# Chunk-wise loads of the activations in the last stage, with vector-engine additions and rows in another order

## What is computed

```python
top_s, top_pos = lax.top_k(cand_s, PEER_TOPK)
expert = jnp.take_along_axis(cand_i, top_pos, axis=-1)
gate = jax.nn.softmax(top_s, axis=-1)
ue = u[expert]
ve = v[expert]
act = jax.nn.gelu(jnp.einsum('thkd,td->thk', ue, ht))
return jnp.einsum('thk,thkd->td', gate * act, ve)
```

## Time and profile before

| | us |
|---|---|
| median of 3 runs | 2850.15 |
| lowest, highest run | 2846.03, 2854.32 |
| the profiled execution | 2851.25 |
| its span | 2849.5 |
| PE busy (95% of the span) | 2694.0 |
| DVE busy (72%) | 2065.5 |
| POOL busy (50%) | 1415.5 |
| ACT busy (32%) | 904.6 |

### The profile page before, as it was taken

The page is one execution under the profiler, slowest core; times in us unless marked ns, Lnnn a source line. Parts: engine busy times, 40 slices in busy tenths (PEclk is TensorE's granted clock), DMA queues, the critical chain, the costliest instruction groups (busy, mean ns, idle before and its releaser), DMA issues.

```text
span 2849.5 us, 43062 instructions
## 1 busy us (share of the span) xinstructions
PE 2694.0 (95%) x15691; PEld 2359.4 (83%) x15691; DVE 2065.5 (72%) x4758; ACT 904.6 (32%) x1750; POOL 1415.5 (50%) x960
## 2 busy tenths in 40 slices
PE   7999979998999999999999999979999998999998
PEld 6776658998999999999999999757767776777776
DVE  6022263699888989999999953668787777778774
ACT  4222341322222222356666622312222222222222
POOL 1111030446566677765565565535565554656640
PEclk9999989999999999999999999989999999999999
DMA  3101031436777888899999999989999999999993
GB/s 140 45 30 30 23 121 51 126 116 224 247 273 258 285 280 275 281 334 381 382 377 377 384 342 332 340 308 358 349 369 359 330 365 326 352 368 358 354 331 135
DMA packets 301905, 763.34 MB, mean 268 GB/s; under 512 B 22992, under 2 KB 138064, under 8 KB 298960
## 3 DMA queue, kind: packets, MB, share of 16 engines
q0 software_dynamic: 110592, 402.70, 38.4%
q1 hardware_dynamic: 191184, 359.13, 36.6%
HBM read 669.47 MB, written 92.27 MB: 267 GB/s over the span
## 4 chain that ended last, share of the span: by engine, by line
PE 54%; DVE 19%; issue 7%; DMA 4%; POOL 2%; ACT 1%; another core or an unknown queue 0%; SPq 0%; DVEq 0%; ACTq 0%
PE bank L1537 22%; PE bank L1881 20%; PE bank L1845 5%; DVE u_row L1332 4%; DMA g_raw<-g_d 3%; PE bank L1773 2%; PE bank L1756 2%; DVE yg L1467 2%; DVE y L1440 1%; PE wide L1901 1%; POOL w_lo L622 1%; DVE prod L1420 1%; DVE rest_k L1259 1%; DVE ix L1262 1%; DVE eq L1319 1%
## 5 line engine op out<-in xcount | busy, mean ns | idle before, releaser
L1537 PE MATMUL bank<-h_hi,w_hi 128*128 128x320 f32 (+1 forms) x2400 | 574.4, 321 | 16.4 <-POOL w_lo L622 12.8
L1537 PE MATMUL bank<-h_hi,w_lo 128*128 128x320 f32 (+1 forms) x2400 | 557.5, 314 | 0.0
L1537 PE MATMUL bank<-h_lo,w_hi 128*128 128x320 f32 (+1 forms) x2400 | 557.1, 313 | 0.0
L622 POOL TENSOR_TENSOR w_lo<-w_raw,w_hi 128x1024 fp32r<-128x1024 f32 x144 | 368.2, 2557 | 336.1 <-ACT w_hi L910 280.7
L1332 DVE CUSTOM_DVE_ANT_0 u_row<-wide,u_row 128x1024 f32<-128x1024 f32 x384 | 450.3, 1221 | 80.1 <-DMA u_row<-in_u_rows,ids 73.2
L684 POOL DMA_INDIRECT d_row<-in_v,ids x256 | 368.2, 1438 | 277.3 <-DVE yg L1467 231.6
L1881 PE MATMUL bank<-v_hi,a_hi 128*128 128x512 f32 x1272 | 408.1, 403 | 73.2 <-DVE y L1440 59.9
L631 POOL DMA_INDIRECT u_row<-in_u_rows,ids x384 | 391.3, 1019 | 111.5 <-issue 76.8
L1537 PEld LDWEIGHTS bank<-h_hi,w_hi 128*128 128x128 f32 x2400 | 401.1, 190 | 22.9 <-POOL w_lo L622 14.6
L1537 PEld LDWEIGHTS bank<-h_lo,w_hi 128*128 128x128 f32 x2400 | 406.7, 189 | 3.9
L1537 PEld LDWEIGHTS bank<-h_hi,w_lo 128*128 128x128 f32 x2400 | 405.5, 189 | 3.9
(11 more groups left out here) (213 smaller groups left out, 3682.5 us busy)
## 6 DMA issues: line engine op xcount, KB each, us to landing
w_raw<-in_u SPq DMA_DIRECT2D x128, 512.0 KB
v_raw<-in_v SPq DMA_DIRECT2D x128, 512.0 KB
act_d<-act_st SPq DMA_DIRECT2D x128, 320.0 KB
g_d<-g_st SPq DMA_DIRECT2D x20, 2048.0 KB
a_raw<-act_d SPq DMA_DIRECT2D x32, 768.0 KB
g_raw<-g_d SPq DMA_DIRECT2D x32, 768.0 KB
w_raw<-in_w_q SPq DMA_DIRECT2D x32, 512.0 KB
a_raw<-act_d SPq DMA_DIRECT2D x32, 512.0 KB
```

The lines of the kernel that those rows point to most:

```text
L622: nc.gpsimd.tensor_tensor(w_lo[:, s % 2, :], w_raw[:, s % 2, :], w_hi[:, s % 2, :], ALU.subtract).then_inc(lo_done, 1)
L1537: ins = pe.matmul(banks[h][:, 0:n], lhs[:, part], rhs[:, k, h * n:(h + 1) * n], start=(k == 0 and lhs is lhs_hi and rhs is h_hi), stop=(k ...
```

## The change

It has four parts, all in the second product.

1. `a_raw` is now eight places of one chunk each, in the same memory as the two places of four chunks before. `load_a(n)` loads the activations of product n alone, when product n - 8 has been gated (`pd_done`), and signals its own semaphore. `gated(n)` waits for that semaphore, and once for four chunks for the gates. The gates still come four chunks at a time. Instead of 64 loads there are 256.
2. SP's list: the five loads of `y` go from ahead of the stage to behind the first unit of group 0, and of each group's last four loads of `v` two more go ahead of the last unit.
3. `add_half` goes from the end of DVE's iteration n % 8 == 2 to the place right behind `lower_a(n)`.
4. Rows of `d_row`: in place of an even spread, `ROWS_PRODUCT` gives the number for each of a group's 16 iterations, 17 in all, 7 in iterations 0 to 7 and 10 in 8 to 15. POOL's gathers follow the same function.

```diff
+ROWS_PRODUCT = (0, 0, 0, 1, 1, 2, 2, 1, 2, 2, 0, 2, 2, 1, 0, 1)
+AR = 8
...
 def rows_added(n):
-    return min(max((n - 3) * VT * P // (HALVES * GT - 20), 0), VT * P)
+    full, m = divmod(n, 2 * GT)
+    return min(max(full * sum(ROWS_PRODUCT) + sum(ROWS_PRODUCT[:m]) - ROWS_PRODUCT[0], 0), VT * P)
...
-        a_raw = [at(f"a_raw{s}", 186 + 6 * s, [P, VJ, WA]) for s in range(2)]
+        a_raw = at("a_raw", 186, [P, AR, WA])
...
             def load_a(n):
-                j, w, s = GT * (n // 4) + VJ * (n % 2), half_width(n // 2), n % 2
-                t0 = n // 2 % 2 * WA
-                sp.dma_start(a_raw[s][:, :, 0:w], act_d[j:j + VJ, :, t0:t0 + w]
-                             .rearrange("j p t -> p j t")).then_inc(a_in[s], 16)
+                h, j = n // GT, GT * (n // (2 * GT)) + n % GT
+                w, t0 = half_width(h), h % 2 * WA
+                if n >= AR:
+                    sp.wait_ge(pd_done, n - AR + 1)
+                sp.dma_start(a_raw[:, n % AR, 0:w], act_d[j, :, t0:t0 + w]).then_inc(a_in[n % AR], 16)
...
-            def load_unit(n):
-                sp.wait_ge(pd_done, VJ * (n - 1))
-                load_a(n)
-                load_g(n)
+            def load_products(n0):
+                for n in range(n0, n0 + VJ):
+                    load_a(n)
+                sp.wait_ge(pd_done, n0 - VJ)
+                load_g(n0 // VJ)
...
             sp.wait_ge(uh_gate, 1)
-            for i in range(DT):
-                sp.dma_start(y[i][:, :], x1_d[i]).then_inc(y_in, 16)
             sp.wait_ge(row_used, ROWS)
...
-                load_unit(4 * g + 2)
-                load_unit(4 * g + 3)
+                n0 = 2 * GT * g
+                load_products(n0 + 2 * VJ)
+                if g == 0:
+                    for i in range(DT):
+                        sp.dma_start(y[i][:, :], x1_d[i]).then_inc(y_in, 16)
+                load_products(n0 + 3 * VJ)
                 for j in more[:VJ]:
                     load_v(j)
                 if more:
-                    load_unit(4 * g + 4)
-                for j in more[VJ:VR]:
+                    load_products(n0 + 4 * VJ)
+                for j in more[VJ:]:
                     load_v(j)
                 if more:
-                    load_unit(4 * g + 5)
-                for j in more[VR:]:
-                    load_v(j)
+                    load_products(n0 + 5 * VJ)
...
                 if n % VJ == 0:
-                    dve.wait_ge(a_in[s], 16 * (n // (2 * VJ) + 1))
                     dve.wait_ge(g_in[s], 16 * (n // (2 * VJ) + 1))
+                dve.wait_ge(a_in[n % AR], 16 * (n // AR + 1))
...
                 lower_a(n)
+                h = n // GT
+                if n % GT == 2 and h:
+                    if h == 1:
+                        dve.wait_ge(y_in, 16 * DT)
+                    for q in range(TT[(h - 1) % 2]):
+                        add_half(h - 1, q)
                 done = n - RA - 1
...
                     add_row(k)
-                h = n // GT
-                if n % GT == 2 and h:
-                    if h == 1:
-                        dve.wait_ge(y_in, 16 * DT)
-                    for q in range(TT[(h - 1) % 2]):
-                        add_half(h - 1, q)
```

More of the change, by code:

```diff
@@ L351, in build @@
         yd_done = sem("yd_done")
-        a_in = [sem("a_in0"), sem("a_in1")]
+        a_in = [sem(f"a_in{k}") for k in range(AR)]
         g_in = [sem("g_in0"), sem("g_in1")]
@@ L562, in _ @@
                     sp.wait_ge(act_out[1], 16 * GT // 2)
-                    load_a(k - 2)
+                    for n in range(VJ * (k - 2), VJ * (k - 1)):
+                        load_a(n)
                 elif k == 4:
@@ L1420, in gated @@
                 V.tensor_tensor(prod[:, n % 2, 0:w].rearrange("p (b t) -> p b t", t=TW),
-                                a_raw[s][:, j, 0:w].rearrange("p (b t) -> p b t", t=TW),
+                                a_raw[:, n % AR, 0:w].rearrange("p (b t) -> p b t", t=TW),
                                 g_raw[s][:, 0:w // TW, j * TW:(j + 1) * TW], ALU.mult).then_inc(pd_done, 1)
```

## The result

The change made the kernel slower: 2864.28 us median (2859.57 to 2872.29, 8 runs) against 2849.76 us of the kernel before (2846.03 to 2856.52, 8 runs), a ratio of 1.0045 with a 95% interval of 1.0031 to 1.0058. The prediction said 2798 us and gave "slower" 0.12. The profiled execution of the change took 2865.24 us, its span is 2863.5 us.

A forecast was written before the change was run, and what follows sets the result against it. PE sets the second product's pace, stalled by DVE's late additions, with the DMA limit near. Groups going from 64.25 to 60.8 us give 48 us over 14, with group 0 53 us: 2851.25 to 2798 us, range 2766 to 2842.

The forecast's parts named there:

- Part 3 (with part 4), additions behind `a_lo`: Second product, group starts: PE's stall and low clock go, 5.2 us for each of 14 groups, 73 us.
- PE's floor: Second product: groups take 59 us, bound by PE alone; as a rival 2772 us, chance 0.18.
- The lateness of the gates, put at nothing: Second product: late gates cost little, 3.58 us once in the steady groups and 13.3 in group 0; 0 us counted.
- Part 2, SP's list: Second product: 5 us gained in group 0; two earlier `v` loads cost 0 to 2 us a group, taken as 0.
- Part 1, chunk-wise loads: Second product's activations: gates arrive 3 us sooner and the hole at 139 GB/s fills; 0 us counted directly.
- rival of the many small transfers: Activation loads: twelve more fixed parts of 1.3 us a group, served one after the other, 159 us more, 3010; chance 0.03.
- Part 4, rows in pairs: DVE's iterations 4 to 11: two rows make 3.3 us against PE's 4.1 us a product, so it fits.
- rival "rows in pairs": Second product: paired rows arrive late, so DVE is late for `a_lo`; 25 us slower, 2876; chance 0.09.
- The DMA bound: Second product: a group's 22.5 MB take 60.0 to 60.5 us at the best rates groups reached, 375 and 372 GB/s.
- The rival of the full DMA: Second product: the DMA is already full at 358 GB/s, 62.9 us a group, 24 us gained, 2827; chance 0.20.
- The signs: Wrong if groups exceed 62.5 us, PE waiting for `a_lo` and DVE for `g_raw` or `d_row`, or short halves stall at their start.
- theory D: Kernel before, second product: DVE's order of work makes PE's 3.5 us stall at a group's start, while the DMA keeps up.

The follow-up runs named there:

- s3_late_spread: Chunk-wise loads, even rows and spread `v` loads, but additions at the old place at the iteration's end: `c2_spread` without part 3; 2830.91 us, ratio to before 0.9955.
- c2_spread: The change with even rows, the last two `v` loads behind the last unit again, and a group's `v` loads spread in SP's list; 2790.31 us, ratio to before 0.9815.
- l4_late_add: The change with part 3 alone taken back: additions again at the end of iteration n % 8 == 2; 2861.78 us, ratio to before 1.0052.
- o1_add: The kernel before with part 3 alone, the additions right behind `a_lo`; 2845.05 us, ratio to before 0.9988.
- s1_after_spread: The change with a group's `v` loads spread in SP's list and nothing else, rows still in pairs; 2777.08 us, ratio to before 0.9769.
- l1_units: The change with part 1 alone taken back: activations again in units of four chunks; 2883.49 us, ratio to before 1.0125.
- l3_rows: The change with part 4 alone taken back: rows of `d_row` spread evenly again; 2849.03 us, ratio to before 1.0006.
- o2_add_rows: The kernel before with parts 3 and 4, additions behind `a_lo` and rows in pairs, units and SP's list as before; 2864.03 us, ratio to before 1.0074.
- s2_before_spread: The kernel before with a group's `v` loads spread in SP's list and nothing else; 2844.02 us, ratio to before 0.9999.
- c1_chunks_add: The change with even rows and the last two `v` loads behind the last unit again; 2832.71 us, ratio to before 0.9957.
- c3_gentle: `c1_chunks_add` with 17 rows in another pattern, none in iterations 1 and 2, no pairs next to each other, `v` loads not spread; 2847.99 us, ratio to before 1.0012.

## Why the prediction was wrong, by its own steps

- **Part 3 (with part 4), additions behind `a_lo`: right in its mechanism, wrong in its condition.** `s3_late_spread` against `c2_spread` measures it where the gates are in time: 2830.91 - 2790.31 = 41 us, 2.9 for each of 14 groups, and pairs of rows bring 13 more: 54 us of the predicted 73 for the floor. In the change (`l4_late_add`) and on the kernel before alone (`o1_add`) part 3 brought 0. The step said that the stall goes because DVE would come to the additions 4.8 us earlier; it did not ask what DVE would then wait for. In `o1_add` it waits in front of `prod`. With both in force and the gates in time, PE's floor is the one predicted, 59.0 us for a group.
- **The lateness of the gates, put at nothing: this step failed.** Part 1 said "Late gates cost little now", and part 2 said of the two `v` loads "cost between 0 and 2 us for a group; I take 0 because the DMA bound below contains it". The sum then added nothing to the DMA's time for a group. But a bound on the rate says how long all bytes of a group take, and not when one load lands that stands behind others. In the change the gates of product 16 landed 22.6 us after they were asked for and those of product 20 after 19.0, which is 3.7 and 5.6 us late; DVE waited 123.6 us for gates. The same bytes with the same rows in `s1_after_spread` had them after 12.8 and 6.9 us, with one wait in group 0, and the time was 2777 us: 21 us under the forecast, where the change was 66 us over it.
- **Part 2, SP's list: too small, but not the main loss.** For the two `v` loads it counted the bytes ahead of the gates, 1 MB at 188 GB/s, and not the wait: SP holds the loads of the last unit until the places of the two `v` loads are free, and the gates are then asked for 3.8 us after their own condition. Taking this edit back gave 15 us, 8 by the ratios, which is 0.5 to 1 us for a group and inside the 0 to 2 that were named. The larger part came from `v` loads that stood in the list of before already, four of them in one burst between the units, and the prediction did not question that. The prediction read SP's waits as room to spare, and did not look at the loads that stand behind them.
- **Part 1, chunk-wise loads: right, undervalued.** Counted as 0 us directly; `l1_units` shows 19 us in the change. That they would fill the hole at 139 GB/s did not come true: in the change the hole is deeper, 44 to 234 GB/s for 12 us, since each chunk waits for DVE and `v` waits behind the chunks. The rival of the many small transfers (0.03) had the wrong sign. The rule of the Trainium skill that it leaned on ("DMA: Bandwidth & Descriptors", Measured: transfers of 1 MiB and more) did not hold for loads of 128 and 192 KB with others in flight: the fastest version has them at 382 GB/s.
- **Part 4, rows in pairs: "fits" was right only with the gates in time.** The rival "rows in pairs" named the effect, DVE waits for rows; they are there (53.6 us), and `l3_rows` takes 15 us off. But its price was for a ring of six places and the place in POOL's queue, and `s1_after_spread` has the same rows in the same places with 1.8 us of waiting. So the waits for rows follow the late gates. The likely way is that DVE, stopped by the gates, frees no places, and the gathers then come together; that is argued and was not tried. What pairs cost with the list of before, 19 us in `o2_add_rows`, is the other half of it: they bring gathers together where the gates are under way.
- **The DMA bound.** I weighed two limits, 59.0 by PE and 60.0 by the best rate of a group, and took 60.8 since they "don't overlap perfectly". They do: a group of the fastest version takes 59.0 us (its `v` loads at 2158.73 and 2217.74 are 59.0 apart). The best rate of a group had been taken for a bound of the DMA, though the prediction itself said that the rate followed the demand. The rival of the full DMA (358 GB/s, which the Trainium skill, in the section Where 436 GB/s comes from, gives as the bound between HBM and SBUF for a core) is refuted by 375 to 383 GB/s over the stage; that nothing else ran beside this core may be why, and was not tried.
- **Group 0** gained little: 78.8 us in place of 80, with DVE still waiting 13.1 us for gates. Of the predicted 5 us (its text counts four rows less, its sum three) about 1 came.
- **The signs** that were to show the forecast wrong are in the profile but for one: groups are over 62.5 us and DVE waits for `g_raw` and `d_row`, but PE waits for `y` (58.8 us), not for `a_lo`. So the late gates reach PE by way of the additions.

What stays open: the move of the `y` loads was in no run by itself; in no trace do DVE's additions wait longer than 1.8 us for that load. Why `s2_before_spread` gains nothing at all is only argued: there DVE's late additions (53.6 us of PE's waits) hold PE, as theory D says.

## What to carry to other kernels

A fix of one engine's order pays only if the data can follow the shorter period. Ahead of such a change, take for each load the time from its issue to its use, in an ordinary period and in the worst one, and check it against the new period. In a list that an engine issues in order, as SP does here, look at what each load stands behind: the bytes ahead of it, and also the condition of every entry ahead of it; bulk loads with early free places belong where the DMA has little to do, not right in front of a load that somebody waits for. Where undoing each of several edits gives a little, try the missing piece that they all compete for before giving any of them up.

## What was unexpected of the hardware

The rate that the core's DMA reached depended on when it was asked: 339 to 345 GB/s in stretches of 200 us of the change, 375 to 383 with the same bytes in another order (`s1_after_spread`), at shares of 0.94 or 0.95 and of 1.03 or 1.04. And versions near the edge fall in and out of the late regime within one execution, as `c1_chunks_add` does. The spread of their runs may come from the same: 2836 to 2866 us for `l3_rows` and 2829.53 to 2859.70 for `c3_gentle` (10 runs each), but 2775.05 to 2780.43 for `s1_after_spread` (4 runs), and 2837 to 2853 for the kernel before (22 runs). So a spread of 1% is a reason to look for a transfer that arrives just in time.
